# Block-1 attention as one woven stream of recurrence and sparse attention, with the probabilities computed a second time in transposed form

## What is computed

```python
p_cmp = masked_softmax(sc, cmp_end[None, :] <= t[:, None]); o_cmp = p_cmp @ vc      # 31 compressed blocks
p_sel = masked_softmax(ss, pos_sel <= t); o_sel = p_sel @ v_sel   # n_sel = all 8 blocks: plain causal attention
p_win = masked_softmax(sw, win_mask);     o_win = p_win @ v_win   # window 512 >= sequence: causal too
o = g[..., 0:1] * o_cmp + g[..., 1:2] * o_sel + g[..., 2:3] * o_win     # g = sigmoid(gate_logits)
```

```python
q = silu(hq); f = lb + (1 - lb) * sigmoid(hf); k = 1 - f; b = cumsum(log f) in the chunk
o = (q * exp(b)) @ S + attn @ v          # attn[t,s] = sum_d q[t,d] k[s,d] exp(b[t,d] - b[s,d]), s <= t
S = exp(b_last) * S + (k * exp(b_last - b)).T @ v
o = rms_norm(o) * silu(hg)
```

## Time and profile before

| | |
|---|---|
| median of 3 runs | 2338.64 us (2336.73 to 2338.94) |
| profiled execution, its own time | 2338.64 us |
| its span | 2336.8 us |
| PE busy | 2077.8 us, 89% |
| DVE, ACT, POOL busy | 42%, 35%, 30% |
| granted PE clock, mean | 0.948 of full speed |
| first 20% of the span, PE busy in tenths of a slice | 58767676 |
| block-1 attention, from the first half of HQ 0 to `w_out` | 426.8 us, of it PE busy 301.4 |

### The profile page before, as it was taken

One profiled execution on the slowest core, in us unless ns is written; L12 is line 12 of the kernel. 1 busy time (PEld: TensorE's weight loads), 2 busy tenths in 40 slices (PEclk: granted clock), 3 DMA queues, 4 the chain that ended last, 5 costly groups with the idle time before them and its releaser, 6 DMA issues.

```text
span 2336.8 us, 24822 instructions
## 1 busy us (share of the span) xinstructions
PE 2077.8 (89%) x9211; PEld 1596.9 (68%) x9211; DVE 987.1 (42%) x1443; ACT 809.9 (35%) x1215; POOL 710.9 (30%) x299
## 2 busy tenths in 40 slices
PE   5876767669999999989988999999989979999997
PEld 3645454457888887756646888888656647888885
DVE  5355556564453625445553321324444443232233
ACT  4232333333432424434344322324344433222223
POOL 2210101103353434422213434434222213443531
PEclk9987888889999999999989999999999989999997
DMA  7101100012232332311102323333211112333321
GB/s 207 38 26 27 27 19 28 19 28 81 82 108 81 100 94 78 99 46 45 55 28 72 109 82 108 99 86 95 63 46 46 53 29 84 111 89 95 109 82 48
DMA packets 322429, 164.79 MB, mean 71 GB/s; under 512 B 18243, under 2 KB 320902, under 8 KB 322182
## 3 DMA queue, kind: packets, MB, share of 16 engines
q1 hardware_dynamic: 321824, 162.64, 24.8%
q10 hardware_dynamic: 486, 0.56, 0.1%
HBM read 160.56 MB, written 2.10 MB: 70 GB/s over the span
## 4 chain that ended last, share of the span: by engine, by line
PE 78%; DVE 12%; ACT 7%; issue 2%; ACTq 0%; POOL 0%; DMA 0%; DVEq 0%
PE accs L1332 22%; PE accs L1334 21%; PE accs L1333 21%; PE S L1482 1%; PE TT L1287 1%; DVE W L1245 1%; DVE W L1230 1%; PE O L1449 1%; PE O L1565 1%; DVE W L1240 1%; PE TT L1527 1%; PE S L1549 1%; PE S L1431 1%; ACT W L818 1%; ACT W L816 1%
## 5 line engine op out<-in xcount | busy, mean ns | idle before, releaser
L569 POOL TENSOR_TENSOR wlo<-raw,whi 128x1024 fp32r<-128x1024 f32 x295 | 710.7, 2412 | 1588.7 <-ACT whi L594 1588.7
L1332 PE MATMUL accs<-Xh,whi 128*128 128x512 f32 x1448 | 604.0, 417 | 2.3 <-POOL wlo L569 2.3
L1333 PE MATMUL accs<-Xl,whi 128*128 128x512 f32 x1448 | 577.3, 399 | 0.0
L1334 PE MATMUL accs<-Xh,wlo 128*128 128x512 f32 x1448 | 577.1, 399 | 0.0
L594 ACT ACTIVATE whi<-raw 128x1024 fp32r<-128x1024 f32 x297 | 313.7, 1060 | 236.2 <-PE accs L1334 221.8
L1332 PE MATMUL accs<-Uh,whi 128*128 128x512 f32 x880 | 347.5, 395 | 8.2 <-DVE Ul L1184 4.6
L1333 PE MATMUL accs<-Ul,whi 128*128 128x512 f32 x880 | 345.2, 392 | 0.0
L1334 PE MATMUL accs<-Uh,wlo 128*128 128x512 f32 x880 | 344.9, 392 | 0.0
L1332 PEld LDWEIGHTS accs<-Xh,whi 128*128 128x128 f32 x1448 | 282.7, 195 | 74.3 <-issue 19.0
L1333 PEld LDWEIGHTS accs<-Xl,whi 128*128 128x128 f32 x1448 | 282.0, 195 | 63.9 <-issue 8.2
L1334 PEld LDWEIGHTS accs<-Xh,wlo 128*128 128x128 f32 x1448 | 279.8, 193 | 61.5
(11 more groups left out here) (235 smaller groups left out, 1851.6 us busy)
## 6 DMA issues: line engine op xcount, KB each, us to landing
raw<-in_w_ff_dram SPq DMA_DIRECT2D x128, 512.0 KB
raw<-in_w_in_dram SPq DMA_DIRECT2D x71, 512.0 KB
raw<-in_w_gate_up_dram SPq DMA_DIRECT2D x44, 512.0 KB
raw<-in_w_down_dram SPq DMA_DIRECT2D x16, 512.0 KB
raw<-in_w_o_dram SPq DMA_DIRECT2D x16, 512.0 KB
raw<-in_w_down_dram SPq DMA_DIRECT2D x8, 384.0 KB
W<-in_x_dram SPq DMA_DIRECT2D x4, 512.0 KB, 6.1
...
```

The lines of the kernel that those rows point to most:

```text
L569: pool.tensor_tensor(wlo[:, slot], raw[:, slot], whi[:, slot].bitcast(F32), ALU.subtract)\
L1332: mmul(y, whi[:, slot, k], xh[:, k], start=(i == 0), stop=False)
L1333: mmul(y, whi[:, slot, k], xl[:, k], start=False, stop=False)
L1334: last = mmul(y, wlo[:, slot, k], xh[:, k], start=False, stop=(i == len(ks) - 1))
```

## The change

Four things change in block-1 attention; everything after `w_out` begins is left as it was.

1. The order. A round is now written out by hand as one stream: recurrence steps, attention steps and projection halves alternate. The units HF and HQ of a round are made in the round before it (for round 0, ahead of the loop), so hq, hb and hk become double buffers; q4 keeps two pairs instead of four.
2. The probabilities. `n1` makes the scores once for the row maximum and the row sum alone: its exponential is written back over `S`. `n2a` makes, for each query, the shift c = -max - ln(sum) - (-ln gate) and splits it into three bf16 terms. `n2b` turns these into 6 rows (four small bf16 matmuls into `M`, copied to `crow`). `n3` makes the scores again, transposed (128 keys against all later queries), adds the shift by a bf16 matmul with 6 rows (`sel`, `crow`) and a transposed mask, and one exponential writes the finished, gated and transposed probabilities `PTb`. `n4` multiplies by the values, one key block at a time. `nn`, `nt` and `nv` go.
3. The recurrence works on `TT` alone (`hd`, `hl`, `ho`), no longer on `S` and `O`; its levels' exponential is split into two halves of 256 columns with signs +1 and -1, so the negated copy `nb` goes. `ha` becomes `ha1` and `ha2`, and its `on` becomes `hn1` and `hn2`.
4. The gates are kept as -ln(gate): `ga` is maximum, exponential, ln(1+x) in place of exponential, add, reciprocal. The early load of constants leaves out the rotary tables and fetches 384 more columns by a second DMA; `params` has one more cast, of 384 columns.

```diff
@@ block1
-    attn = [("mmA", u(C_HQ)), ("nq2", 0, R_QN)]
+    attn = half(C_HF, 0, 0, [("nq2", 0, R_QN)]) + half(C_HF, 0, 1, [("fg", 0)])
+    attn += half(C_HQ, 0, 0, [("fg2", 0)]) + half(C_HQ, 0, 1, [("fg3", 0), ("silu", "hq", 0)])
     for i in range(4):
-        hq, hf, hi, hg = (u(c + 128 * i) for c in (C_HQ, C_HF, C_HI, C_HG))
-        halves = [[("mmA", hq)]] * (i > 0) + [[("mmB", hq), ("silu", "hq")], [("mmA", hf), ("silu2", "hq")], [("mmB", hf), ("fg",)],
-                                              [("mmA", hi), ("fg2", i)], [("mmB", hi), ("fg3",), ("vt",)]]
-        attn += weave(halves, nsa_slots(i) + [[("vt2", "hv")]])
-
-        attn += [("mmA", hg), ("ha", i), ("hu", i), ("hd", i), ("hl", i, 0), ("mmB", hg), ("silu", "hg"), ("hl", i, 1)]
-        if i < 3:
-            q = u(C_Q, pair=i + 1)
-            attn += [("mmA", q), ("silu2", "hg"), ("hl", i, 2), ("hl", i, 3), ("mmB", q), ("nq", i + 1), ("hl", i, 4), ("nq2", i + 1, R_QN)]
-        else:
-            attn += [("hl", i, 2), ("silu2", "hg"), ("hl", i, 3), ("hl", i, 4)]
-        attn += [("hl", i, 5), ("hl", i, 6), ("hl", i, 7), ("ho", i), ("on", "hgrn", i, 4 + i)]
+        nxt = i < 3
+        attn += [("ca", i)] + half(C_HI, i, 0) + [("silu2", "hq", i), ("n1", i, 0, 0)]
+        attn += [("ha1", i)] + half(C_HI, i, 1, [("vt",)]) + [("cb", i), ("hd", i), ("n1", i, 0, 1), ("cv", i)]
+        attn += half(C_HG, i, 0) + [("ha2", i), ("vt2", "hv"), ("n1", i, 0, 2), ("hl", i, 0)]
+        attn += half(C_HG, i, 1, [("silu", "hg", i)]) + [("n1", i, 0, 3), ("hu", i), ("n2a", i, 0), ("hl", i, 1), ("silu2", "hg", i)]
+        attn += [("n1", i, 1, 0)] + (quarter(i + 1, 0) if nxt else []) + [("n2b", i, 0), ("hl", i, 2), ("n3", i, 0, 0)]
+        attn += [("n1", i, 1, 1)] + (quarter(i + 1, 1, [("nq", i + 1)]) if nxt else []) + [("n3", i, 0, 1), ("hl", i, 3), ("n4", i, 0, 0)]
+        attn += [("n1", i, 1, 2)] + (half(C_HF, i + 1, 0, [("nq2", i + 1, R_QN)]) if nxt else []) + [("n3", i, 0, 2), ("hl", i, 4), ("n4", i, 0, 1)]
+        attn += [("n1", i, 1, 3)] + (half(C_HF, i + 1, 1, [("fg", i + 1)]) if nxt else [])
+        attn += [("n2a", i, 1), ("n3", i, 0, 3), ("hl", i, 5), ("n4", i, 0, 2)] + ([("fg2", i + 1)] if nxt else [])
+        attn += (half(C_HQ, i + 1, 0) if nxt else []) + [("n2b", i, 1), ("hl", i, 6), ("n4", i, 0, 3), ("n3", i, 1, 0)] + ([("fg3", i + 1)] if nxt else [])
+        attn += [("hl", i, 7), ("n3", i, 1, 1), ("n4", i, 1, 0)]
+        attn += (half(C_HQ, i + 1, 1, [("silu", "hq", i + 1)]) if nxt else []) + [("n3", i, 1, 2), ("ho", i), ("n4", i, 1, 1)]
+        attn += [("n3", i, 1, 3), ("hn1", i), ("n4", i, 1, 2), ("n4", i, 1, 3), ("hn2", i, 4 + i), ("mixo", i)]
@@ ScalarE
 ga:
-                    A(hq, hq, ACT.Exp, scale=-1.0).then_inc(sems["si_e"], 1)
+                    A(gq, gq, ACT.Exp, scale=-1.0).then_inc(sems["act"], 1)
+                    A(gq, gq, ACT.Ln, bias=1.0).then_inc(sems["ga_ok"], 1)
 n1:
-                        A(prs[qb % 2][:, g, 0:n], S[:, g, 0:n], ACT.Exp, bias=nm[:, g:g + 1], accum_out=sums[:, g:g + 1])
+                        A(S[:, g, 0:n], S[:, g, 0:n], ACT.Exp, bias=nmx[:, c + g:c + g + 1], accum_out=sme[:, c + g:c + g + 1])
+n2a:                A(lsm, sme[:, 8 * a:8 * a + 8], ACT.Ln).then_inc(sems["n_ln"], 1)
+n2b:                A(crow[:, item[2]], M[0:6, :], ACT.Copy).then_inc(sems["M_act"], 1)
+n3:                 A(PTb[kb % 2][:, :, 0:n], S[:, :, 0:n], ACT.Exp).then_inc(sems["S_act"], 1)
 hl:
-                        A(HD[:, a % 2], HD[:, a % 2], ACT.Exp).then_inc(sems["hl_e"], 1)
+                        A(sides_of[:, :, 0, :], sides_of[:, :, 0, :], ACT.Exp, scale=-1.0).then_inc(sems["act"], 1)
+                        A(sides_of[:, :, 1, :], sides_of[:, :, 1, :], ACT.Exp).then_inc(sems["hl_e"], 1)
@@ VectorE
 ga:
-                    TS(hq, hq, 1.0, None, ALU.add).then_inc(sems["dve"], 1)
-                    dve.reciprocal(hq, hq).then_inc(sems["ga_ok"], 1)
+                    TS(gq, gq, -80.0, None, ALU.max).then_inc(sems["ga_x"], 1)
+n2a:                TTn(cc, mx, lsm, ALU.subtract)      # then -ln(gate) off, and three bf16 terms: 6 instructions of 8 columns
 hl:
-                        TTn(HD[:, a % 2].rearrange("p (n h t) -> p n h t", h=2, t=m), sides(nb, hb, m), seams(nb, hb, m), ALU.subtract)
+                        TTn(HD[:, a % 2].rearrange("p (n t) -> p n t", t=2 * m), b3, b3[:, :, m - 1:m].to_broadcast([P, T // (2 * m), 2 * m]), ALU.subtract)
-                        TTn(F, sides(hk, hq, m), Dx, ALU.mult).then_inc(sems["hl_f"], 1)
+                        TTn(F, sides(hk[p], hq[p], m), F, ALU.mult).then_inc(sems["hl_f"], 1)
 params:
+                    CP(masks[:, 4:7, :], cst[:, LATE:LATE + 3 * P].rearrange("p (a n) -> p a n", n=P)).then_inc(sems["dve"], 1)
@@ TensorE
+                elif kind == "n2b":
+                    pe.wait_ge(sems["n_c"], at("c16"))
+                    for qb in range(NB):
+                        last = mmul(M[0:6, P * qb:P * qb + P], c16[:, a, qb, :], identb, start=True, stop=True)
+                elif kind == "n3":
+                    _, i, a, kb = item
+                    n = T - P * kb
+                    pe.wait_ge(sems["M_act"], at("crow"))
+                    pe.wait_ge(sems["S_act"], at("S_act"))
+                    pe.wait_ge(sems["S_dve"], at("S_dve"))
+                    for g in range(2):
+                        mmul(S[:, g, 0:n], kts[a][hrows(g), P * kb:P * kb + P], q4[hrows(g), i % 2, P * kb:T], start=True, stop=False)
+                    for g in range(2):
+                        mmul(S[:, g, 0:n], sel[g], crow[:, a, P * kb:T], start=False, stop=False)
+                    for g in range(2):
+                        last = mmul(S[:, g, 0:P], identb, m_causT, start=False, stop=True)
+                elif kind == "n4":
+                    pe.wait_ge(sems["S_act"], at(f"pt{kb % 2}"))
+                    for g in range(2):
+                        last = mmul(O[64 * g:64 * g + 64, P * kb:T], vs["vw" if a else "vs"][:, kb, 64 * g:64 * g + 64],
+                                    PTb[kb % 2][:, g, 0:T - P * kb], start=False, stop=(a == 1 and kb == 3))
```

More of the change, by code:

```diff
@@ L153, in events_of, with marks_of @@
     return EVENTS[kind]
+def marks_of(item):
+    kind = item[0]
+    if kind == "mixo":
+        return dict(mixed="ul")
+    if kind == "n2a":
+        return dict(c16="n_c")
+    if kind == "n2b":
+        return {"crow": "M_act", "c16_read": "M_fill"}
+    if kind == "n3":
+        return {f"pt{item[3] % 2}": "S_act", "crow_read": "S_fill"}
+    if kind == "vt2":
+        return {"v_" + item[1]: "M_dve"}
+    if kind == "ha2":
+        return dict(hk_ok="M_dve", hd_read="M_fill")
+    if kind == "cb":
+        return dict(pct_a="S_act", pct_d="S_dve")
+    if kind == "fg3":
+        return dict(hb_ok="si_ok")
+    if kind == "silu2":
+        return {item[1] + "_ok": "si_ok"}
+    if kind == "hu":
+        return dict(hs_ok="T_dve")
+    return {}
 def mm(unit):
@@ L182, in halves_of @@
     return out
-def nsa_slots(i):
-    blocks = [(i, a, qb) for a in range(2) for qb in range(NB)]
-    s = [[("ca", i)], [("cb", i), ("ns",) + blocks[0]]]
-    for n in range(len(blocks) + 1):
-        slot = [("cv", i)] if n == 0 else [("nt",) + blocks[n - 1]]
-        if n < len(blocks):
-            slot.append(("nn",) + blocks[n])
-        if n + 1 < len(blocks):
-            slot.append(("ns",) + blocks[n + 1])
-        if n and blocks[n - 1][2] == NB - 1:
-            slot.append(("nv", i, blocks[n - 1][1]))
-        s.append(slot)
-    return s + [[("mixo", i)]]
 def sb_slots(j):
@@ L212, in produced @@
 def produced(items):
-    return tuple(it[-1] for it in items if it[0] in ("mixo", "on"))
+    return tuple(it[-1] for it in items if it[0] in ("mixo", "on", "hn2"))
 def block1():
@@ L341, in over @@
             self.base[name] = self.base.get(name, 0) + n
+        for name, key in marks_of(item).items():
+            self.base[name] = self.base[key]
         self.base[self.me] = self.base.get(self.me, 0) + self.own
@@ L402, in build @@
         eps = con("cols")[:, 0:1]
-        identb, m_sb, m_causal, m_chunk = (masks[:, n, :] for n in range(4))
+        identb, m_sb, m_causal, m_chunk, m_causT = (masks[:, n, :] for n in range(5))
+        sel = [masks[0:6, 5 + g, :] for g in range(2)]
+        nmx, sme, lsm, cc = nsm[:, 0:16], nsm[:, 16:32], nsm[:, 32:40], nsm[:, 40:48]
         lb, omlb = small[:, 0:4], small[:, 4:8]
@@ L1465, in stage @@
                 elif kind == "hd":
-                    pe.wait_ge(sems["si_ok"], at("si_ok"))
-                    pe.wait_ge(sems["S_act"], at("S_act"))
-                    pe.wait_ge(sems["S_dve"], at("S_dve"))
+                    p = item[1] % 2
+                    pe.wait_ge(sems["si_ok"], at("hq_ok"))
+                    if begun("T_act"):
+                        pe.wait_ge(sems["T_act"], at("T_act"))
+                    if begun("T_dve"):
+                        pe.wait_ge(sems["T_dve"], at("T_dve"))
```

(4 more changed lines are left out.)

430 lines of the change are left out of this document (239 added, 191 removed).

## The result

The changed kernel takes 2342.32 us (median of 15 runs, 2339.07 to 2348.83), the kernel before 2338.09 (2333.33 to 2340.08) beside it: a ratio of 1.002 (1.0012 to 1.0028). It is 0.2% slower. I had said 2302, and faster with a chance of 0.78.

What follows compares the result with a forecast made beforehand. PE was taken as bound by chains between engines that it waits for; 70.5 us work, 23.0 waits and 5 clock loss made 98.5 a round. With the last round, start and gates, 36.9 us less: 2302 us, range 2280 to 2330 (0.58).

Steps and rivals of the forecast that it cites:

- PE work: Attention rounds: scores made twice, shift and n2b added, 40 transposes out; 6.1 us more, 70.5 us a round at full clock.
- The shift's matmul: In n3, bf16 with 6 rows: one pass of 0.23 us per 512 columns and group, 1.15 us a branch.
- the second product: In n3, the scores made a second time: 3.4 us of PE work a branch at full clock.
- Waits: PE stands still at nine places a round, 23.0 us in sum instead of 34.3, longest at hl 1, 5.4.
- The exponential back into PSUM: In n1, written back over S: taken at no extra cost, between 0.06 us less and 0.3 more on 16 of them.
- the rival: S becomes the bound: 1 us more ahead of each of 16 score turns, waiting 39 a round, 2362 us; chance 0.14.
- the 14 us of bare waits forecast: Last round: the first three waits (11.5 us) stay, the later ones stand bare at some 14 us.
- Ahead of the rounds: Two projection halves more ahead of the first ca, 12.4 us in all; gates 2.7 less, extra cast 0.7 more.
- The gates: Before the transposes of vt2: a logarithm of 0.63 us replaces the reciprocal of 3.35, 2.7 us less.
- Clock: Attention rounds: loss to half speed falls from 10.5 to 5 us with less waiting, ends 0 and 10.5; last round 5.5.
- given back: Rival: shorter waits met by PE at half clock; 28 us waiting and 8.5 clock loss a round, 2335; chance 0.11.
- the outer range: Whole kernel: 2268 to 2348 us, leaving out a tenth at either end; clock 5 us either way fits in.

Runs made afterwards that it cites:

- x11: Changed kernel, order alone: n4, n1 and HF's second half ahead of hl 4, HQ's first half ahead of hl 5, n2a and hl 6 later; 2322.58 us.
- x10: Changed kernel, order alone: hl 1 moved behind the second branch's n1 and half of the next Q pair, hl 2 behind the first n3; 2315.75 us.

## Why the prediction was wrong

*PE work*: right to about a microsecond a round. 70.5 forecast, 69.5 measured (in 1 us windows 7.0 more than before, for the 6.1 forecast; the last round 49.9 for 53.0). The shift's matmul took 0.60 us for a pair of 512 columns, where I took 0.46 between 0 and 1.06, and the second product 6.1 a round for 6.8.

*Waits*: right in sum and mostly in place. 24.1 for 23.0; `cb` 4.02 for 4.3, `hl` 1 5.61 for 5.4, `hl` 4 3.25 for 2.6, `hl` 5 5.20 for 4.9; the second `n1` has 0.3 for 1.8, and the first 1.3 that I hadn't counted. (Reading out a row sum, which I took at 0.1 us, is 0.19 in the earlier trace rows.) In the last round 25.8 for 25.5. The exponential back into PSUM costs nothing more: 0.66 us for 512 columns, 0.69 into SBUF before. `S` did not become the bound: in round 2 its turns are 3.9 us beside `cb`. So the rival is out for the first three rounds, though the Trainium skill's Perfetto Trace Analysis, section Matmuls, by its rule that groups rotate through banks, would have made it the likely one. In the last round the turns do count: with few projection halves left, `n3` waits 8.2 us there for the exponentials of `n1` on `S`, part of the 14 us of bare waits forecast.

```profile
PE S L1522 <- ACT S L750: 8.2, 3, 3.1
```

*Ahead of the rounds*: right. The first `ca` is at 119.42; by the forecast 116.23 + 6.0 - 2.0 = 120.2. The gates gave 2.8 us at `vt2` for the 2.7 forecast.

*Clock*: this is the step that failed. I scaled the old loss of 10.5 with the share of waiting and took 5, with ends 0 and 10.5; measured were 12.3, outside of both ends, and 21.5 in the last round for 5.5. In sum 58.2 for 20.5, 37.7 us. With 3.7 us more behind `w_out`, which I had at nothing, 2302 becomes 2343; measured 2342.32. (The other terms are off by 3.8 us at most and nearly cancel.) The old loss was mis-sized too: in 1 us windows it was 12.5 in round 2, and after the change it is 12.2, so there it didn't follow the waiting at all. The runs show why scaling can't do: x11 has 19.4 us of idle time and loses 16.4, x10 has 20.9 and loses 7.7, and the same 23.6 us piece of a round costs 3.5 us more or not. A wait of 1.2 us with only thin products behind it cost 7.8. What sets the loss of a whole round stays open.

The *given back* rival (2335) was the nearest, and the time lies in its range: it named the mechanism, a PE at half clock behind each shorter wait, but put the loss at 8.5 a round, not above the old one, and the waiting at 28 where 24.1 came. The forecast's place for its bounds was wrong as well: I took it that less waiting can't raise the loss. It can: x11, with 4.7 us less idle time in round 2 than the changed kernel, loses 4.1 more. That the time is inside the outer range, up to 2348, is luck: the 5 us either way that I gave the clock don't cover its 7 in a round and 16 in the last.

A round of the forecast's length can be seen in x10: 98.1 us, idle 20.9, clock 0.90, of which the loss is 7.7.
